# Dense stage of a streaming encoder step: U's products in three rounded passes, fewer buffers, one tile's sums kept in PSUM

## The chip, the cores and the metric

One core of one Trainium2 chip runs the whole program in one launch. The metric is the device time of that launch in microseconds (us), the median of the runs taken. The core has five engines that run side by side, each with its own instruction queue in program order: TensorE (PE, with its weight loads shown as PEld), VectorE (DVE), ScalarE (ACT), GpSimd (POOL) and SyncE (SP). They meet only through semaphores. Transfers that SP and POOL issue run on 16 shared DMA engines.

## The reference, cut to what matters

The program computes one layer: RMSNorm, two kinds of attention, a gated merge, and then a PEER block, a retrieval over 16384 one-neuron experts. Only the PEER block matters here:

```
xn = rmsnorm(x)                                 # 1024 features
e, g = top-16 experts and softmax weights per head, 8 heads     # 128 experts per token
h = u[e] . xn                                   # hidden value of each chosen expert
a = gelu(h) * g
out = sum over e of a * v[e];  y = rmsnorm_final(x + out)
```

There are nine tiles of 128 tokens. `peer_u` and `peer_v` are 16384 x 1024 in float32. The final sums of all tiles, and the keys and values of the attentions, are outputs.

## The kernel before, in words

The stages before the last one (projection, attention, merge, routing) take the first 1905 us. The last stage is the function `dense`, and the change lies there, but for two small things: the early loads in the stage before it, and the list of buffers that are carried over.

`dense` does two jobs at once, for eight of the nine token tiles.

The **dense job** (four tiles, 512 tokens) multiplies by all experts. There are 128 blocks of 128 experts. For each block b, `hidden` (line 2466) forms the 128 x 512 hidden values on PE: eight matmuls of 128x512 in float32 over the feature chunks of `xd`. ACT applies Gelu (line 2448), giving a tile `A`. DVE multiplies `A` by the gates from `G` (line 2375, function `gate`), which are zero for tokens that did not choose the expert. Four blocks make a group (32 groups). `values` (line 2474) multiplies a group's four `A` tiles by V: eight chunks per group (four token tiles times two halves of the features), each four matmuls into one of four PSUM banks. DVE adds each finished chunk into `qacc` in SBUF (line 2384, function `take`). PE's order is: `hidden` of block b, then two chunks of `values` of the group before.

The **fetched job** (four tiles, 128 tokens each) gathers, for each token column slot, one row of u and v per partition. POOL issues one indirect transfer of 1 MB per slot (line 2315) into a ring of eight slots. DVE multiplies the u half with `xn` and sums it (line 2353, `products`), ACT applies Gelu to two columns (line 2438), DVE scales by the gate weight (line 2362) and adds the v half into the tile's sum (line 2367, `add_rows`), then frees the slot. There are 128 slots per tile, 512 in all.

Both jobs are woven into one **body step** per block, 128 in all. DVE's queue for block b (function `body`, line 2386) is: `gate` of block b-1, two `take`s, `products` of two slots, `add_rows` of the two slots before, `products` of two, `add_rows` of two. So each step holds four slots of the fetched job. ACT's step is: small Gelu, Gelu of the block, small Gelu. All engines hold eight steps in the body of a loop (line 2250). A tile of the fetched job is 32 steps; DVE's and ACT's loops end there and `tile_done` finishes the tile. The eight steps of the first body are written out; the other fifteen bodies run in four loops, one per tile, so a loop is left for the last time at each tile's end.

SP (line 2258) loads U blocks into four buffers `ub`, V into two sets of four, and the gates of a group (1 MB) into one of two buffers `gb`. The first four U blocks and V blocks were loaded already in the stage before. A U buffer is free again when PE's `hidden` of the block four earlier is done. At the stage's end SP stores `qacc`.

Of the kernel before, what the change touches and what calls it, by code (L numbers as in the profile page):

```python
# [1332 lines left out]
def decide(nc, a, o, software, acc, aw, row_v, ring, w_o, dense_in):  # L1333
# [27 lines left out]
    with ExitStack() as ctx:  # L1361
# [76 lines left out]
        with nc.Block() as block:  # L1438
            @block.sync
            def _(sp):  # L1440
# [128 lines left out]
                for j in range(4):  # L1569
                    sp.dma_start(ring[:, j].rearrange("p (c q) -> p c q", q=P), a["u_blocks"][j]).then_inc(early_in, 16)  # L1570
                    sp.dma_start(ring[:, 4 + j], a["v_blocks"][j]).then_inc(early_in, 16)
# [5 lines left out]
                sp.wait_ge(early_in, 192)  # L1577
# [622 lines left out]
def dense(nc, a, o, soft, early, dense_in):  # L2200
# [7 lines left out]
    LEAD = 2 * DENSE  # L2208
    with ExitStack() as ctx:
# [9 lines left out]
        xn, acc = dense_in.xn, [dense_in.acc, sb("d_acc1", [P, D])]  # L2219
        gf = sb("d_gf", [P, D])  # L2220
        idx8 = [sb(f"d_idx8{u}", [P, SL], I32) for u in range(2)]
        h, ge, aw = (sb(f"d_{n}", [P, P]) for n in ("h", "ge", "aw"))
# [3 lines left out]
        HB, VB, SPARE = 0, 2, 6  # L2226
        wide = lambda b: ps[:, b:b + 2, :].rearrange("p b n -> p (b n)")

        tabs, rows_in, qacc_in = sem("d_tabs"), sem("d_rows_in"), sem("d_qacc_in")
        gf_in = sem("d_gf_in")  # L2230
        u_in = [sem(f"d_u_in{j}") for j in range(GB)]
        v_in, g_in = [sem(f"d_v_in{u}") for u in range(2)], [sem(f"d_g_in{u}") for u in range(2)]
# [23 lines left out]
        with nc.Block() as block:  # L2256
            @block.sync
            def _(sp):

                def u_rows(b, j):  # L2260
                    if not (number(b) and b < GB):
                        sp.wait_ge(h_done, b - GB + 1)
                        sp.sem_inc(sp_past, 1)
                    sp.dma_start(ub[j], a["u_blocks"][b]).then_inc(u_in[j], 16)
# [4 lines left out]
                def group(n, u, beside=lambda j: None):  # L2269
                    if not (number(n) and n < 2):  # L2270
                        sp.wait_ge(gated, GB * (n - 1))
                        sp.sem_inc(sp_past, 1)
                    sp.dma_start(gb[u][:], o["G"][bass.ts(n, GB)].rearrange("b p t -> p b t")).then_inc(g_in[u], 16)
                    for j in range(GB):
                        u_rows(GB * n + j, j)
                        if j == 0 and not (number(n) and n < 2):
                            sp.wait_ge(v_done, 2 * DENSE * (n - 1))
                            sp.sem_inc(sp_past, 1)
                        v_rows(GB * n + j, u, j)
                        beside(j)  # L2280

                for j in range(GB):
                    sp.sem_inc(u_in[j], 16)  # L2283
                sp.sem_inc(v_in[0], 16 * GB)
                sp.dma_start(gb[0][:], o["G"][0:GB].rearrange("b p t -> p b t")).then_inc(g_in[0], 16)
                sp.dma_start(gw[:], o["gw"].rearrange("t p s -> p t s")).then_inc(tabs, 16)
                sp.dma_start(idx[:, 1:], o["idx"][1:].rearrange("t p s -> p t s")).then_inc(rows_in, 16)

                def sums(j):
                    if j == 1:  # L2290
                        sp.dma_start(qacc[:], o["ys"][0:DENSE].rearrange("t p d -> p t d")).then_inc(qacc_in, 16)
# [3 lines left out]
                group(1, 1, sums)  # L2295
                with sp.Fori(1, NG // 2) as i:
                    for u in range(2):
                        group(2 * i + u, u)
                for q in range(DENSE):
                    sp.wait_ge(scaled, FETCHED + q + 1)  # L2300
                    sp.dma_start(o["y"][q], qacc[:, q]).then_inc(qy_st, 16)
# [4 lines left out]
            def _(pool):  # L2306
                def gathers(T, g, par):

                    nc.gpsimd.tensor_copy(idx8[par][:], idx[:, T, bass.ts(g, SL)]).then_inc(idx_copied, 1)
# [15 lines left out]
                for T in range(FETCHED):  # L2325
                    halves = P // SL // 4
                    if T == 1:
# [284 lines left out]
```

## Time and profile before

| what | value |
| --- | --- |
| median of 3 runs | 3753.05 us (3747.15 to 3762.25) |
| the profiled execution's own time | 3756.75 us |
| its span, first to last instruction | 3755.0 us |
| mean granted TensorE clock | 0.958 of full speed |
| PE busy | 3435.2 us, 91% of the span |
| DVE busy | 2662.5 us, 71% |
| ACT busy | 890.0 us, 24% |
| POOL busy | 1447.1 us, 39% |
| moved by DMA | 1201.16 MB, mean 320 GB/s |

How to read it: busy shares are averages over the span, and the last stage starts at about 1906 us. Matmuls are pipelined, so two that follow each other overlap in the records; the spacing of their starts tells more than the duration of one. "Idle before" gives the time for which the engine stood still just before an instruction, and the name behind it what ended that. "issue" there means that the profile shows nothing that the engine waited for. A wait of an engine that is not the bottleneck costs nothing.

### The profile page before, as it was taken

The page shows a single profiled execution, that of the slowest core. Times are in us where ns is not written, and L with a number is a line of the kernel's source. Part 1 is how long each engine was busy: PE and PEld are TensorE (multiplying, and loading weights), DVE is VectorE, ACT ScalarE, POOL GpSimd, SP SyncE. Part 2 cuts the span into 40 slices and gives each one's busy share as a digit, 9 for nine tenths or more (in the row PEclk, how much of TensorE's full clock was granted, in tenths as well). Part 3 has the DMA queues.
Part 4 walks back from the last instruction along what each step waited for, and adds up shares of the span by engine and source line. Part 5 has one row for each costly group of instructions (what it writes and reads, how often), then busy time and mean ns, then how long its engine had stood idle before and what let it go on. Part 6 is the DMA issues. An engine that isn't in the chain of part 4 may idle for free.

```text
span 3755.0 us, 45250 instructions
## 1 busy us (share of the span) xinstructions
PE 3435.2 (91%) x14374; PEld 2026.9 (54%) x14374; DVE 2662.5 (71%) x4988; ACT 890.0 (24%) x1844; POOL 1447.1 (39%) x1116
## 2 busy tenths in 40 slices
PE   8998989986889998999549999999999999999998
PEld 7444879884466667677414444444444444444443
DVE  0453887756368755655768888887888888889786
ACT  1452211215122338797100000100001000100001
POOL 0000187740232778874023343333343334333331
PEclk8899999988899999999779999999999999999999
DMA  7898499975887668888679999999999999999994
GB/s 262 342 421 298 136 401 378 378 275 168 322 311 252 170 179 182 193 147 190 205 285 398 406 398 390 398 390 391 409 385 400 406 397 418 401 399 365 387 379 185
DMA packets 470727, 1201.16 MB, mean 320 GB/s; under 512 B 196953, under 2 KB 261897, under 8 KB 391817
## 3 DMA queue, kind: packets, MB, share of 16 engines
q0 software_dynamic: 149776, 679.68, 47.7%
q1 hardware_dynamic: 187200, 498.50, 35.7%
q10 hardware_dynamic: 133568, 20.84, 3.5%
q8 instruction: 80, 1.31, 0.1%
q14 instruction: 103, 0.84, 0.1%
HBM read 1127.33 MB, written 72.61 MB: 320 GB/s over the span
## 4 chain that ended last, share of the span: by engine, by line
PE 32%; DVE 8%; issue 4%; DMA 4%; DVEq 1%; POOL 1%; POOLq 0%
PE d_ps L2482 17%; PE d_ps L2471 15%; DVE d_acc L2367 4%; DMA d_ring<-peer_uv,d_idx 3%; DVE d_ring L2353 3%; DMA out_y<-k_yacc 1%; DVE d_qacc L2384 1%; DVE k_yacc L2367 1%; POOL d_ring L2315 0%; DVE d_aw L2362 0%; DVE d_a L2375 0%; DVE d_qacc L2413 0%; DVEq L2362 0%; DVEq L2353 0%; DVEq L2366 0%
## 5 line engine op out<-in xcount | busy, mean ns | idle before, releaser
L2315 POOL DMA_INDIRECT d_ring<-peer_uv,d_idx x512 | 654.3, 1278 | 1067.1 <-DVEq L2369 964.1
L2471 PE MATMUL d_ps<-k_xd,k_ring 128*128 128x512 f32 x2048 | 907.0, 596 | 74.6 <-SPq L2283 60.4
L2471 PEld LDWEIGHTS d_ps<-k_xd,k_ring 128*128 128x128 f32 x2048 | 391.5, 191 | 569.4 <-issue 508.3
L2353 DVE SCALAR_TENSOR_TENSOR d_ring<-d_ring,k_xn 128x1024 f32<-128x1024 f32 x512 | 605.6, 1219 | 70.2 <-DMA d_ring<-peer_uv,d_idx 39.5
L2482 PE MATMUL d_ps<-d_v,d_a 128*128 128x512 f32 x1024 | 456.9, 600 | 32.5 <-DVE d_a L2375 24.6
L2482 PE MATMUL d_ps<-k_ring,d_a 128*128 128x512 f32 x1024 | 451.7, 594 | 16.1 <-DVE d_a L2375 16.1
L1630 POOL DMA_INDIRECT G<-c_cellg,c_cell x256 | 420.2, 1641 | 116.8 <-issue 90.1
L2367 DVE SCALAR_TENSOR_TENSOR d_acc<-d_ring,d_aw,d_acc 128x1024 f32<-128x1024 f32 x256 | 328.8, 1284 | 49.9 <-DVE d_acc L2367 32.3
L2367 DVE SCALAR_TENSOR_TENSOR k_yacc<-d_ring,d_aw,k_yacc 128x1024 f32<-128x1024 f32 x256 | 328.7, 1284 | 47.8 <-DVE k_yacc L2367 31.7
L2482 PEld LDWEIGHTS d_ps<-d_v,d_a 128*128 128x128 f32 x1024 | 196.3, 193 | 284.7 <-issue 283.4
L2438 ACT ACTIVATE d_ge<-d_h (+1 forms) x256 | 52.1, 203 | 1238.6 <-DVE d_ring L2353 1238.5
L2482 PEld LDWEIGHTS d_ps<-k_ring,d_a 128*128 128x128 f32 x1024 | 195.1, 191 | 262.5 <-issue 262.0
L2142 PE MATMUL c_ps<-c_mT,c_chunk 128*128 128x128 f32 x2048 | 250.2, 283 | 23.6 <-DMA c_chunk<-wq 22.5
L2142 PEld LDWEIGHTS c_ps<-c_mT,c_chunk 128*128 128x128 f32 x2048 | 244.6, 199 | 29.3 <-DMA c_chunk<-wq 24.2
L934 POOL DMA_INDIRECT k_merge<-peer_uv,a_rowu x128 | 168.9, 1319 | 193.7 <-DVE k_rowv L1002 148.1
L2384 DVE TENSOR_TENSOR d_qacc<-d_ps,d_qacc 128x512 f32<-128x512 f32 x256 | 167.5, 683 | 49.0 <-PE d_ps L2482 41.6
L1024 DVE SCALAR_TENSOR_TENSOR k_merge<-k_merge,k_xg 128x1024 f32<-128x1024 f32 x128 | 152.8, 1223 | 51.9 <-DMA k_merge<-peer_uv,a_rowu 47.0
L1094 PE MATMUL a_ps<-a_w_high,k_x_part 128*128 128x256 f32 x896 | 166.9, 288 | 1.8 <-issue 1.7
L1596 POOL DMA_INDIRECT k_ring<-peer_uv,k_rowv x56 | 66.9, 1195 | 219.7 <-DVE k_acc L1800 98.7
L2375 DVE TENSOR_TENSOR d_a<-d_a,d_gb 128x512 f32<-128x512 f32 x128 | 88.5, 691 | 80.3 <-issue 50.2
L1094 PEld LDWEIGHTS a_ps<-a_w_high,k_x_part 128*128 128x128 f32 x896 | 143.2, 196 | 3.0 <-issue 2.6
L1094 PE MATMUL a_ps<-a_w_low,k_x_part 128*128 128x256 f32 x448 | 129.1, 288 | 11.0 <-ACT a_stage L1051 9.1
(382 smaller groups left out, 4442.3 us busy)
## 6 DMA issues: line engine op xcount, KB each, us to landing
c_chunk<-wq SPq DMA_DIRECT2D x128, 512.0 KB
k_ring<-u_blocks SPq DMA_DIRECT2D x128, 512.0 KB, 12.7
s_kc<-sb_kT SPq DMA_DIRECT2D x32, 1024.0 KB, 9.1
s_vc<-sb_v SPq DMA_DIRECT2D x32, 1024.0 KB, 7.3
c_chunk<-w_m SPq DMA_DIRECT2D x64, 512.0 KB
k_ring<-v_blocks SPq DMA_DIRECT2D x64, 512.0 KB, 13.4
d_gb<-G SPq DMA_DIRECT2D x32, 1024.0 KB
d_v<-v_blocks SPq DMA_DIRECT2D x64, 512.0 KB
```

The lines of the kernel that those rows point to most:

```text
L934: pool.indirect_dma_start(out=ring[:, k % RB], out_offset=None, in_=rows, in_offset=bass.IndirectOffsetOnAxis(ap=source[:, k % P:k % P + 1 ...
L1024: nc.vector.scalar_tensor_tensor(ring[:, r], ring[:, r], 1.0, xg[:], ALU.mult, ALU.mult, accum_out=h_sb[:, s:s + 1]).then_inc(freed, 1)
L1094: last = nc.tensor.matmul(out, lhsT(left, k), rhs(right, k), start=(k == 0 and n == 0), stop=(k == KC - 1 and n == 2))
L1630: pool.indirect_dma_start(out=grid, out_offset=bass.IndirectOffsetOnAxis(ap=cell[q][:, s:s + 1], axis=0), in_=cell_g[q][:, s:s + 1], in_of ...
L2142: last = nc.tensor.matmul(ps[:, QUERY[w // 4], (w % 4) * P:(w % 4 + 1) * P], wq[:, c * P:(c + 1) * P], xT[:, c], start=(c == 0), stop=(c = ...
L2315: pool.indirect_dma_start(out=ring[:, b], out_offset=None, in_=a["peer_uv"], in_offset=bass.IndirectOffsetOnAxis(ap=idx8[par][:, b:b + 1], ...
L2353: last = nc.vector.scalar_tensor_tensor(ring[:, b, 0:D], ring[:, b, 0:D], 1.0, xn[T % 2][:], ALU.mult, ALU.mult, accum_out=h[:, bass.ds(co ...
L2367: nc.vector.scalar_tensor_tensor(acc[T % 2][:], ring[:, b, D:], aw[:, bass.ds(col + n, 1)], acc[T % 2][:], ALU.mult, ALU.add).then_inc(sum ...
L2375: nc.vector.tensor_tensor(A[u][j][:], A[u][j][:], gb[u][:, j], ALU.mult).then_inc(gated, 1)
L2384: nc.vector.tensor_tensor(part, ps[:, VB + c % 4, :], part, ALU.add).then_inc(v_taken, 1)
L2471: last = nc.tensor.matmul(ps[:, HB + x % 2, :], ub[j][:, k], xd[:, k].rearrange("p t q -> p (t q)"), start=(k == 0), stop=(k == KC - 1))
L2482: last = nc.tensor.matmul(ps[:, VB + c % 4, :], A[u][j][:, q * P:(q + 1) * P], vb[u][j][:, half * 512:half * 512 + 512], start=(j == 0), s ...
```

## The change

- U's products run in three passes in the type float32r. `x_high` is a rounded copy of the dense tokens, `x_low` what is missing to the full value; both are made once at the stage's start (ACT copies, DVE subtracts, 128x2048 at a time, two of each). For every block ACT makes `u_high` (128x1024, `high`) and DVE makes `u_low` = U - `u_high` (128x1024, `low`). PE then does eight times (`u_high` x `x_high`, `u_high` x `x_low`) and, once `u_low` is there, eight times `u_low` x `x_high`. There is one `u_high` and one `u_low`, so ACT's `high` of block b waits until PE has used and DVE has read the last one, and DVE's `low` of b waits until PE has finished b-1.
- Two U buffers in place of four; one is free when `low` has read it. Only two U blocks are loaded in the stage before.
- The gates lie in two buffers of half a group each (512 KB), in the space of the two U buffers.
- `A` lies in the space of `xd`, which is spent once `x_high` and `x_low` are made.
- The fourth token tile's two chunks (c = 6, 7) stay in PSUM over all 32 groups and are added to the tile once, at the end, so `take` runs for six chunks of a group and not eight. The bank pair that ACT's `square_sum` wrote to is gone; it writes to a spent `xn` buffer.
- Slot lists and gate weights of the fetched job are loaded per tile by POOL, half a tile ahead, and not all at once by SP.

```diff
-        ub = [early[:, j].rearrange("p (c q) -> p c q", q=P) for j in range(GB)]
+        ub = [early[:, s].rearrange("p (c q) -> p c q", q=P) for s in range(2)]
+        u_high, u_low = (sb(f"d_u_{part}", [P, KC, P], F32R) for part in ("high", "low"))
+        x_high, x_low = (sb(f"d_x_{part}", [P, KC, Q], F32R) for part in ("high", "low"))
-        gb = [sb(f"d_gb{u}", [P, GB, Q]) for u in range(2)]
-        A = [[sb(f"d_a{u}{j}", [P, Q]) for j in range(GB)] for u in range(2)]
-        qacc = sb("d_qacc", [P, DENSE, D])
+        gb = [early[:, 2 + s].rearrange("p (b t) -> p b t", t=Q) for s in range(2)]
+        A = [[x_all[:, GB * u + j] for j in range(GB)] for u in range(2)]
+        qacc = sb("d_qacc", [P, DENSE - 1, D])
 # SP
                 def u_rows(b, j):
-                        sp.wait_ge(h_done, b - GB + 1)
-                    sp.dma_start(ub[j], a["u_blocks"][b]).then_inc(u_in[j], 16)
+                    sp.wait_ge(u_low_done, b - 1)
+                    sp.dma_start(ub[j % 2], a["u_blocks"][b]).then_inc(u_in[j % 2], 16)
 # POOL, half way through each tile
                         pool.dma_start(xn[(T + 1) % 2][:], o["xn"][T + 1]).then_inc(xn_in, 16)
+                        pool.dma_start(idx[:, (T + 1) % 2], o["idx"][T + 1]).then_inc(xn_in, 16)
+                        pool.dma_start(gw[:, (T + 1) % 2], o["gw"][T + 1]).then_inc(xn_in, 16)
 # DVE
+                def low(b, j):
+                    dve.wait_ge(u_high_done, b + 1)
+                    if not (number(b) and b == 0):
+                        dve.wait_ge(h_done, b)
+                    nc.vector.tensor_tensor(u_low[:], ub[j % 2], u_high[:].bitcast(F32), ALU.subtract).then_inc(u_low_done, 1)
                 def take(n, c):
+                    if c >= KEPT:
+                        return
 # DVE body, after gate of b-1 and before the takes
+                        low(b, j)
 # ACT
+                def high(b, j, round):
+                    act.wait_ge(u_in[j % 2], 16 * (round + 1))
+                    if not (number(b) and b == 0):
+                        act.wait_ge(high_used, b)
+                        act.wait_ge(u_low_done, b)
+                    nc.scalar.activation(u_high[:], ub[j % 2], ACT.Copy).then_inc(u_high_done, 1)
 # ACT body, ahead of the first small Gelu
+                        high(b, j, 4 * k + x // 2)
 # PE
                     for k in range(KC):
-                        last = nc.tensor.matmul(ps[:, HB + x % 2, :], ub[j][:, k], xd[:, k].rearrange("p t q -> p (t q)"), start=(k == 0), stop=(k == KC - 1))
+                        for n, x_part in enumerate((x_high, x_low)):
+                            last = nc.tensor.matmul(ps[:, HB + x % 2, :], u_high[:, k], x_part[:, k], start=(k == 0 and n == 0), stop=False)
+                    last.then_inc(high_used, 1)
+                    pe.wait_ge(u_low_done, b + 1)
+                    for k in range(KC):
+                        last = nc.tensor.matmul(ps[:, HB + x % 2, :], u_low[:, k], x_high[:, k], start=False, stop=(k == KC - 1))
                     last.then_inc(h_done, 1)
```

## Rows read from the trace of the kernel before

**Rows 1.** The page: busy time by engine; the chain's share by engine.

```profile
PE 3435.2 (91%) x14374; PEld 2026.9 (54%) x14374; DVE 2662.5 (71%) x4988; ACT 890.0 (24%) x1844; POOL 1447.1 (39%) x1116
PE 32%; DVE 8%; issue 4%; DMA 4%; DVEq 1%; POOL 1%; POOLq 0%
```

**Rows 2.** Windows of the dense stage: busy us by engine, clock, DMA share, GB/s.

```profile
2908.00:3018.00 110.00, 110.00 (x258) 48.77 (x257) 95.67 (x137) 9.21 (x25) 42.86 (x36) 1.00 1.01 407
2457.00:2569.00 112.00, 110.18 (x257) 48.56 (x256) 94.79 (x136) 9.20 (x25) 42.80 (x36) 1.00 0.99 395
```

**Rows 3.** Timeline of PE: start, length, instruction, count (16: half a step).

```profile
2430.94 7.03 PE L2471 MATMUL d_ps<-k_xd,k_ring 128*128 128x512 f32 x16
2437.80 7.03 PE L2482 MATMUL d_ps<-k_ring,d_a 128*128 128x512 f32 x16
```

**Rows 4.** Timeline of DVE over one step, from gate to gate, same columns.

```profile
2430.81 0.69 DVE L2375 TENSOR_TENSOR d_a<-d_a,d_gb 128x512 f32<-128x512 f32 x1 [0.23 <-DVE d_acc L2367]
2431.42 1.28 DVE L2384 TENSOR_TENSOR d_qacc<-d_ps,d_qacc 128x512 f32<-128x512 f32 x2
2432.62 1.22 DVE L2353 SCALAR_TENSOR_TENSOR d_ring<-d_ring,k_xn 128x1024 f32<-128x1024 f32 x1
2433.76 0.08 DVE L2353 DVE_READ_ACCUMULATOR d_ring<-d_ring,k_xn  x1
...
2443.93 0.69 DVE L2375 TENSOR_TENSOR d_a<-d_a,d_gb 128x512 f32<-128x512 f32 x1 [0.23 <-DVE d_acc L2367]
```

**Rows 5.** Chain that ended last, 2400 to 2600 us: start, length, what.

```profile
2474.01 5.93 issue
2481.96 4.10 DVE d_ring L2353 x7
```

**Rows 6.** Timeline of PE, three passes in float32r in the projection.

```profile
440.07 0.62 PE L1094 MATMUL a_ps<-k_x_part,a_w_high 128*128 128x512 f32 x2
...
440.75 0.62 PE L1094 MATMUL a_ps<-k_x_part,a_w_high 128*128 128x512 f32 x2
```

**Rows 7.** Lines that split high and low parts: ns min/median/max; and a 128x1024 copy.

```profile
L944 DVE TENSOR_TENSOR a_w_low<-k_merge,a_w_high x11: 2284/2292/2312, 395.9 to 796.4; 128x2048 fp32r<-128x2048 f32 x11
L1056 ACT ACTIVATE a_w_high<-k_merge x11: 1915/1917/1923, 393.9 to 761.2; 128x2048 fp32r<-128x2048 f32 x11
L1949 ACT ACTIVATE c_mT<-c_y 128x1024 f32<-128x1024 f32 x8 | 8.3, 1043 | 14.3 <-DVE c_y L1675 14.3
```

**Rows 8.** Waits of DVE, 2034 to 3690 us: total, times, longest.

```profile
DVE d_a L2375 <- issue: 50.2, 8, 6.8
DVE d_qacc L2384 <- PE d_ps L2482: 18.2, 31, 3.6
DVE d_ring L2353 <- DMA d_ring<-peer_uv,d_idx: 10.9, 8, 2.8
```

**Rows 9.** Timeline of DVE at a loop's return: a slow one, one of third tile.

```profile
2480.15 0.69 DVE L2375 TENSOR_TENSOR d_a<-d_a,d_gb 128x512 f32<-128x512 f32 x1 [6.41 <-issue]
...
2926.17 0.69 DVE L2375 TENSOR_TENSOR d_a<-d_a,d_gb 128x512 f32<-128x512 f32 x1 [0.71 <-DVE k_yacc L2367]
```

**Rows 10.** Timeline of DVE at the stage's start, first gathered slots.

```profile
1917.19 1.22 DVE L2353 SCALAR_TENSOR_TENSOR d_ring<-d_ring,k_xn 128x1024 f32<-128x1024 f32 x1 [11.10 <-DMA d_ring<-peer_uv,d_idx]
1935.02 1.23 DVE L2353 SCALAR_TENSOR_TENSOR d_ring<-d_ring,k_xn 128x1024 f32<-128x1024 f32 x1 [1.39 <-DMA d_ring<-peer_uv,d_idx]
```

**Rows 11.** PE after a long stand, and clock (before last two) of the window.

```profile
2709.25 4.05 PE L2482 MATMUL d_ps<-d_v,d_a 128*128 128x512 f32 x5 [6.21 <-DVE d_a L2375]
2704.00:2712.00 8.00, 2.75 (x4) 1.21 (x5) 3.59 (x6) 0.00 (x0) 0.60 (x2) 0.61 1.02 421
2480.99 1.55 PE L2482 MATMUL d_ps<-d_v,d_a 128*128 128x512 f32 x3 [1.82 <-DVE d_a L2375]
```

**Rows 12.** The page: U's transfers of 512 KB, us from issue to landing.

```profile
k_ring<-u_blocks SPq DMA_DIRECT2D x128, 512.0 KB, 12.7
```

**Rows 13.** Line of the gate: ns min/median/max, first and last start.

```profile
L2375 DVE TENSOR_TENSOR d_a<-d_a,d_gb x128: 683/691/693, 1931.8 to 3715.5; 128x512 f32<-128x512 f32 x128
```

More of the change, by code:

```diff
@@ L2197, in _, with dense @@
                 scores_of(NT - 1)
-def dense(nc, a, o, soft, early, dense_in):
+def dense(nc, a, o, soft, spent_acc, early, dense_in):
     GB = 4
@@ L2280, in group @@
                         beside(j)
[L2282 removed]
+                for j in range(2):
                     sp.sem_inc(u_in[j], 16)
                 sp.sem_inc(v_in[0], 16 * GB)
[L2285 to L2287 removed]
+                for s in range(2):
+                    gates(0, s)
@@ L2296, in _ @@
-                with sp.Fori(1, NG // 2) as i:
+                group(0, 0, beside=sums)
+                group(1, 1)
+                with sp.Fori(1, NG // 2 - 1) as i:
                     for u in range(2):
                         group(2 * i + u, u)
+                group(NG - 2, 0)
+                group(NG - 1, 1, last=True)
+                sp.wait_ge(scaled, FETCHED - 1)
+                sp.dma_start(xn[0][:], o["ys"][DENSE - 1]).then_inc(held_in, 16)
                 for q in range(DENSE):
@@ L2419, in tile_done @@
                     if T + 1 < FETCHED:
-                        dve.wait_ge(xn_in, 16 * (T + 1))
+                        dve.wait_ge(xn_in, 48 * (T + 1))
                         dve.wait_ge(acc_in, 16 * (T + 1))
+                dve.wait_ge(x_high_done, KC)
+                for half in range(2):
+                    part = slice(half * KC // 2, (half + 1) * KC // 2)
+                    nc.vector.tensor_tensor(x_low[:, part], x_all[:, part], x_high[:, part].bitcast(F32), ALU.subtract).then_inc(x_low_done, 1)
                 bodies(dve, body, tile_done)
@@ L2428, in _ @@
                     take(NG - 1, c)
+                dve.wait_ge(held_in, 16)
+                for half in range(2):
+                    dve.wait_ge(v_done, 2 * DENSE * NG)
+                    part = xn[0][:, half * 512:(half + 1) * 512]
+                    nc.vector.tensor_tensor(part, ps[:, HELD + half, :], part, ALU.add).then_inc(v_taken, 1)
                 for q in range(DENSE):
-                    finish(FETCHED + q, qacc[:, q])
+                    finish(FETCHED + q, totals[q])
             @block.scalar
@@ L2458, in tile_done, with hidden @@
                     square_sum(T, acc[T % 2][:], summed, P * (T + 1))
+                for half in range(2):
+                    part = slice(half * KC // 2, (half + 1) * KC // 2)
+                    last = nc.scalar.activation(x_high[:, part], x_all[:, part], ACT.Copy)
+                    last.then_inc(x_high_done, KC // 2)
                 bodies(act, body, tile_done)
                 for q in range(DENSE):
-                    square_sum(FETCHED + q, qacc[:, q], v_taken, LEAD + 2 * DENSE * (NG - 1) + 2 * q + 2)
+                    square_sum(FETCHED + q, totals[q], v_taken, LEAD + KEPT * (NG - 1 if q < DENSE - 1 else NG) + (2 * q + 2 if q < DENSE - 1 else 2))
             @block.tensor
             def _(pe):
-                def hidden(b, x, j, round):
-                    pe.wait_ge(u_in[j], 16 * (round + 1))
+                def hidden(b, x, j):
+                    if number(b) and b == 0:
+                        pe.wait_ge(x_high_done, KC)
+                        pe.wait_ge(x_low_done, 2)
+                    pe.wait_ge(u_high_done, b + 1)
                     if not (number(b) and b < 2):
```

96 lines of the change are left out of this document (56 added, 40 removed).

## The prediction, made before the result was known

> **What bounds the kernel now.** I read the page first, then the windows of the last stage, then the two timelines of one body step, and last the chain and the waits. The page makes PE the bound: busy 91% against 71% for DVE, and the chain that ended last lies 32% on PE and 8% on DVE [rows 1]. The share of DVE is an average over stages, so the reader should next look at the dense stage alone. In a stretch of 110 us PE is busy all of it, DVE 95.67 us, and the DMA engines are at a share of 1.01 with 407 GB/s [rows 2]. Three resources are near their end together.
>
> The two timelines settle which one is first. PE's half step for U, 16 records, starts at 2430.94 and the next half at 2437.80 [rows 3]: 6.86 us, so 0.43 us for each record, and 13.72 us for a step of two halves. DVE's step runs from the gate at 2430.81 to the gate at 2443.93 [rows 4]: 13.12 us, and the idle time in it (0.23 us before a gate) follows DVE's own instructions. So DVE's step is a chain of DVE work that is only 0.60 us shorter than PE's. DVE has a second cost: when its loop returns, the gate starts after 6.41 us of idle time that nothing outside explains [rows 9], and the chain shows it as 5.93 us of "issue" between pieces of DVE work [rows 5]. It happens 8 times for 50.2 us together [rows 8]. In the third tile's loop the return costs 0.71 us [rows 9]. Eight steps with a slow return are 8 x 13.12 + about 6.4 = 111.4 us, eight steps of PE 109.8 us. The window of 112 us spans eight steps with such a return, and PE is busy only 110.18 us of it [rows 2]. DVE's four loops return 11 times, three times each but for the first tile's with two; without the third tile that leaves the 8. So in three of four tiles DVE is already the bound by 1 to 2 us in 110; only in the third tile is PE. That is the opposite of what the page suggests.
>
> **The change, part by part.**
>
> *PE.* A step's U half is now 8 x 3 products of 128x512 in float32r. The projection does just this: two products of one sort and one of the other repeat from 440.07 to 440.75 [rows 6], 0.68 us for three, so 8 x 0.68 = 5.44 us in place of 6.86. PE's step falls from 13.72 to 12.30 us; 128 x 1.42 = 182 us less PE work. The V half is the same. On the path this is worth only what DVE now waits for PE. DVE waits 18.2 us for chunks inside the stage [rows 8]; that is all that can be given back, and I take all of it.
> By the Trainium skill (FP8 and Floating Point Precision, TensorE Precision Notes) full float32 takes four passes through the array, of high and low parts; three of four would make U's half 5.15 us and the saved PE work 219 us. The row's 5.44 us for three passes is measured, and it decides.
>
> *DVE, added.* `low` is a 128x1024 subtraction from SBUF and SBUF. The same operation on 128x2048 takes 2.29 us [rows 7], and a 128x1024 instruction keeps DVE for 1.14 us, from 2432.62 to 2433.76 [rows 4]. Half of 2.29 is 1.15. I take 1.14: 128 x 1.14 = 146 us. Its two waits are resolved in the queue while the gate runs, as those of the takes are, which follow the gate with no idle time [rows 4]. From both sides: 0.60 us (a 128x512 one, from 2431.42 to 2432.62 for two) would be 77 us, with an idle time like the gate's 0.23 on top, 1.37 us, 175 us.
>
> *DVE, removed.* Two of eight takes per group go, 64 in all. Two takes hold DVE from 2431.42 to 2432.62 [rows 4], 0.60 us each: 64 x 0.60 = 38 us less. The last two, added at the end, are as long as the two that they replace: nothing.
>
> *DVE's step.* 13.12 + 1.14 - 0.30 = 13.96 us, against 12.30 for PE. DVE becomes the bound everywhere, by 1.66 us a step.
>
> *The waits that are added.* `low` of b waits for `u_high` of b and for PE's b-1. Behind it on DVE stand the takes and the four slots, so its lateness would cost in full. ACT makes `u_high` (about 1.04 us, as the 128x1024 copy [rows 7]) right after the small Gelu that follows DVE's last `products`. DVE then still has `add_rows` of two slots and the gate, over 3.5 us, against 1.3 us for ACT: hidden. PE's b-1 was done before the Gelu that DVE's gate of b-1 waited for: nothing. Behind `high` on ACT stand the small Gelu and the block's Gelu, which have some 3 us of room. Between 0 and 0.5 us a step (64 us) for such slips; I take 0.
> PE does the high passes before `low` is done, the last eight products (1.8 us) behind it, then 6.86 us of V. That ends about 9 us after `low`, some 5 us before the next takes want the chunks.
>
> *Startup.* The splitting of x takes two copies of 1.92 and two subtractions of 2.29 us [rows 7], and then the first `low`: 9.6 us after the stage's start. DVE waits 11.10 us there for its first slot anyway [rows 10]. If that cover were gone, it would cost 5.7 us of DVE. In the first four steps DVE also waits for slots, 1.39 us before one product [rows 10] and longer before others; three `low`s, 3.4 us, vanish in it. I count 4 us.
>
> *Loads.* A U block is now fetched once `low` of two blocks earlier is done, and ACT wants it nearly two steps later, 25 us. It lands in 12.7 us by the page's median [rows 12]. SP issues more evenly than before. With the DMA engines near their limit [rows 2] it may be late now and then: 0 to 15 us, taken as 0. POOL issues two more small loads in each of three tiles, behind a slack that eight slots of lead give: 0. A longer step lowers the demand on the DMA engines, which should give back some of the 10.9 us that DVE waits for slots [rows 8]; with the stalls in the middle of a tile I take 8 us.
>
> *The loop's return.* DVE's loop grows by some twenty instructions. The three quick returns of the third tile can become slow: 3 x 5.7 = 17 us (6.41 less 0.71 [rows 9]); all could also become quick, 8 x 5.7 = 46 us less. I take the 17, since three of four loops are slow now and the loop only grows.
> The Trainium skill (Runtime: NRT & Kernel Launch, Instruction fetch mechanics) says that a taken branch to a target outside the two blocks of instructions held on chip stalls for their fetch. The trace agrees in kind, with 6.41 us, and the rule also speaks for a longer loop being worse.
>
> *TensorE's clock.* While DVE's loop returns, PE now stands still for over 6 us, since `low` comes behind the return. In the trace before, after a stand of 6.21 us the granted clock is 0.61 on average over the window around it, which is the lower level of 1.2 GHz for most of it; stands of 1.82 us leave it at 2.4 GHz [rows 11]. After each of 11 returns and 3 tile ends PE is then 3 to 7 us behind, and 5 us are covered. I take 11 x 0.5 + 3 x 1 = 8 us; from 0 to 14 x 4 = 56 us.
>
> *Sum.* 146 - 38 - 18 - 4 - 8 + 17 + 8 = +103 us. The profiled execution took 3756.75 us for a span of 3755.0; 3756.75 + 103 = 3860. The median of the runs is 3.7 us lower, so the predicted median is 3856, some 2.7% slower. The tail adds nothing: after the last gate PE has the same 8 chunks to do as now.
>
> **The rivals.**
>
> *A, faster: PE is the bound, and the subtraction goes into DVE's idle time.* For it: PE's 91% and 32% of the chain [rows 1], and the window where PE is busy all of the time [rows 2]. It decides from the point where DVE's step is longer than PE's; it would need DVE's 13.12 us to hold over 1.1 us of wait for PE. Then the limit would be the DMA engines: 5.5 MB a step (four slots, U, V, a quarter of G) at 407 to 421 GB/s is 13.1 to 13.5 us [rows 2, 11], against 14.04 us for a step with all returns now (1783.7 us from the first gate to the last, 127 steps [rows 13]). At 13.2 us that is 127 x 0.84 = 107 us less: about 3650 us. Against it: DVE's unbroken step [rows 4] and its place in the chain [rows 5]. 9%.
>
> *B, little slower: the returns all become quick.* Then +103 - 17 - 46 - 8 = +32, about 3785 us. For it: the third tile does it already [rows 9]. 8%.
>
> *C, much slower: the single `u_high` and `u_low` chain the engines together.* ACT's `high`, PE's passes, DVE's `low` and the Gelu then form one loop that is longer than DVE's step, and PE's gaps bring the lower clock often. It decides once PE's stands in each group pass the lengths of rows 11. With 1 us more per step, +128 us, it is about 3985 us. Against it: the 3.5 us of cover above. 10%.
>
> The likeliest case has 73%. Its own range is 3805 to 3895 us: the 17 us of the returns and the 56 of the clock either way, and 18 us of waits that may not go. The range for 8 in 10 is 3775 to 3915: it takes in B, not A and not most of C. Under 0.5% (19 us) a measurement of this kernel does not tell from no change. Faster by more than that: A and a small rest, 10%. Within it: the low end of B, 5%. Slower: 85%.
>
> **What would show it.** Right: the gates of DVE 13.9 to 14.0 us apart within a loop; `low` at 1.2 us with a spacing of 1.14 us and no idle time before it; the group of U's products with idle time before it that DVE's `u_low` ends; three float32r products in 0.68 us; the line of the takes waiting for PE hardly at all; 8 to 11 "issue" waits of about 6 us on DVE; the chain mostly on DVE in this stage. Wrong: idle time before `low` that ACT's `u_high` or PE ends (C); gates under 13.5 us apart (A); long waits of `high` for U's transfers, which would mean that two buffers are too few; a step where ACT's copy brings a table load with it and Gelu comes late.

## The result, and the profile after

| | before | after |
| --- | --- | --- |
| median | 3750.1 us (3745.92 to 3762.25, 4 runs) | 3869.43 us (3863.2 to 3871.33, 4 runs) |
| the profiled execution's own time, its span | 3756.75, 3755.0 us | 3867.84, 3866.1 us |
| mean granted clock | 0.958 | 0.939 |

The ratio is 1.0308, with a 95% interval of 1.0293 to 1.0324: 119 us slower between the medians, 111 us between the two profiled executions. The forecast had 103 us on the profiled execution and 3856 us for the median.

The page after, in the two lines that answer to [rows 1]: busy time by engine, and the chain's share.

```profile
PE 3334.4 (86%) x15398; PEld 2233.8 (58%) x15398; DVE 2773.1 (72%) x5056; ACT 1032.4 (27%) x1986; POOL 1542.8 (40%) x1122
DVE 28%; issue 10%; PE 9%; DVEq 3%; DMA 1%; ACT 0%; POOL 0%; POOLq 0%; ACTq 0%
```

PE has lost 101 us of busy time and DVE gained 111. DVE's busy share went from 71% to 72% only, while its share of the chain went from 8% to 28%: the shares of busy time don't show who is the bound; the chain does here, and as the experiments show it did before (PE 32%, DVE 8% [rows 1]), where I read past it. The same stretches as in [rows 2], columns as there:

```profile
2908.00:3018.00 110.00, 95.53 (x292) 56.38 (x291) 93.07 (x127) 17.21 (x32) 43.95 (x33) 0.95 0.96 370
2457.00:2569.00 112.00, 98.08 (x301) 58.92 (x300) 94.21 (x132) 16.10 (x30) 44.85 (x33) 0.94 0.95 364
```

PE, busy in all 110 us before, now stands for 14 of them, and the DMA engines move 370 GB/s in place of 407. No engine is full any more, which is how a chain of dependences on one engine looks in such a table: what DVE lacks to 110 us are the small gaps between its own instructions and the return of its loop. DVE after, gates and what follows them (answers to [rows 4]):

```profile
2536.20 0.69 DVE L2407 TENSOR_TENSOR k_xd<-k_xd,k_ring 128x512 f32<-128x512 f32 x1 [0.22 <-DVE k_acc L2392]
2536.81 1.22 DVE L2401 TENSOR_TENSOR d_u_low<-k_ring,d_u_high 128x1024 fp32r<-128x1024 f32 x1
2537.95 1.28 DVE L2418 TENSOR_TENSOR d_qacc<-d_ps,d_qacc 128x512 f32<-128x512 f32 x2
...
2550.48 0.69 DVE L2407 TENSOR_TENSOR k_xd<-k_xd,k_ring 128x512 f32<-128x512 f32 x1 [0.22 <-DVE k_acc L2392]
...
2564.75 0.69 DVE L2407 TENSOR_TENSOR k_xd<-k_xd,k_ring 128x512 f32<-128x512 f32 x1 [0.22 <-DVE k_acc L2392]
2577.91 0.69 DVE L2407 TENSOR_TENSOR k_xd<-k_xd,k_ring 128x512 f32<-128x512 f32 x1 [0.31 <-DVE k_acc L2392]
```

The gates are 14.27 us apart where the step has takes and 13.16 where it has none, one step in four: 13.99 on average, against 13.12. `low` sits between the gate and the takes, costs 1.14 us (2536.81 to 2537.95) and has no idle time before it. PE in the same kernel: the first product of a U half, its last eight, the V half and the next U half:

```profile
2442.60 0.50 PE L2532 MATMUL d_ps<-d_x_high,d_u_high 128*128 128x512 f32 x1 [1.56 <-ACT d_u_high L2486]
...
2446.33 2.08 PE L2536 MATMUL d_ps<-d_x_high,d_u_low 128*128 128x512 f32 x8
2448.26 7.03 PE L2549 MATMUL d_ps<-k_ring,k_xd 128*128 128x512 f32 x16
2455.61 0.50 PE L2532 MATMUL d_ps<-d_x_high,d_u_high 128*128 128x512 f32 x1 [0.33 <-ACT d_u_high L2486]
```

U's half takes 5.66 us in place of 6.86 in [rows 3], and then PE waits 1.56 or 0.33 us for the next `u_high`, which itself waits for DVE: PE's step would be some 12.5 us, and it is given 13.2 to 14.3. The waits of DVE from the first gate to the last, which answer to [rows 8] (total, times, longest; beside the line with "u_high" DVE waits for ACT only at the tiles' ends, 11.4 us as before):

```profile
DVE k_xd L2407 <- issue: 78.2, 11, 11.7
DVE d_qacc L2418 <- PE d_ps L2549: 18.7, 15, 2.7
DVE d_ring L2378 <- DMA d_ring<-peer_uv,d_idx: 1.2, 1, 1.2
DVE d_u_low L2401 <- ACT d_u_high L2486: 0.8, 3, 0.3
```

One return of the loop on DVE, and the same in the chain that ended last (answers to [rows 5, 9]):

```profile
2502.49 1.28 DVE L2392 SCALAR_TENSOR_TENSOR k_acc<-d_ring,k_scores,k_acc 128x1024 f32<-128x1024 f32 x1 [0.26 <-DVE k_acc L2392]
2510.34 0.69 DVE L2407 TENSOR_TENSOR k_xd<-k_xd,k_ring 128x512 f32<-128x512 f32 x1 [6.57 <-issue]
```
```profile
2504.04 6.06 issue
```

Nine of the eleven returns are like it, 5.7 to 7.3 us of idle time. The first tile's two are longer, 10.8 and 11.7 us:

```profile
2269.98 0.69 DVE L2407 TENSOR_TENSOR k_xd<-k_xd,k_ring 128x512 f32<-128x512 f32 x1 [11.65 <-issue]
```

"issue" means that the profile shows nothing that the engine waited for, but the view of the DMA queues shows what arrived meanwhile. Taken over the idle time alone, q14, a queue that carries nothing but instructions, moved one packet of 8 KB in the return at 2510.34 and two in the one at 2269.98; in the quick returns of the third tile in the kernel before it moved none. Its line for each of the two, in this order (queue, packets, MB, share of the 16 engines):

```profile
q14 instruction: 1, 0.01, 0.3%
q14 instruction: 2, 0.02, 0.3%
```

So it is in all 88 returns of the eight kernels here whose DVE loops return: none in the nine quick ones (0.7 us), one or two in the 79 slow ones (3.5 to 12.2 us), two in each of the 17 that are over 10 us. I read the slow returns as stands for DVE's own instructions. No run takes the packets away and keeps the loop, and why a return needs none, one or two is not shown.

PE at the return of 2510.34, and the window around it, with the granted clock ahead of the last two columns:

```profile
2500.34 0.79 PE L2532 MATMUL d_ps<-d_x_high,d_u_high 128*128 128x512 f32 x1 [3.29 <-ACT d_u_high L2486]
2500.92 0.63 PE L2532 MATMUL d_ps<-d_x_low,d_u_high 128*128 128x512 f32 x1
2501.35 0.63 PE L2532 MATMUL d_ps<-d_x_high,d_u_high 128*128 128x512 f32 x1
...
2512.22 3.78 PE L2536 MATMUL d_ps<-d_x_high,d_u_low 128*128 128x512 f32 x8 [5.22 <-DVE d_u_low L2401]
```
```profile
2498.00:2518.00 20.00, 12.45 (x29) 8.79 (x30) 10.59 (x14) 3.77 (x5) 5.59 (x5) 0.66 0.96 358
```

DVE stands 6.57 us. PE stood 3.29 us before it, does 16 products, stands 5.22 us for `u_low`, and its products are 0.43 us apart in place of 0.23: the clock is at 1.2 GHz for two thirds of these 20 us. It is so around each return. From 1960 us on, the low level holds for 203 us after, 42 us before.

The line of the gate closes the account (answers to [rows 13]):

```profile
L2407 DVE TENSOR_TENSOR k_xd<-k_xd,k_ring x128: 684/692/694, 1924.2 to 3825.5; 128x512 f32<-128x512 f32 x128
```

From first to last gate it is 1901.3 us against 1783.7, +117.6. The first gate comes 7.6 us earlier (5.0 of them in stages ahead of this one, which the change hardly touches) and the tail is 1.1 us longer: +111.1, the difference of the spans. The dense stage alone is thus 116 us longer.

### The profile page after: what moved, and what is told of

The parts are those of the page before. It is cut to its first block, busy times and chain, and to the rows that moved or that the text cites. A ratio compares the mean times of both kernels' runs of the same rounds, so it can differ in the third digit from the quotient of the medians.

```text
span 3866.1 us, 48207 instructions
## 1 busy us (share of the span) xinstructions
PE 3334.4 (86%) x15398; PEld 2233.8 (58%) x15398; DVE 2773.1 (72%) x5056; ACT 1032.4 (27%) x1986; POOL 1542.8 (40%) x1122
## 4 chain that ended last, share of the span: by engine, by line
DVE 28%; issue 10%; PE 9%; DVEq 3%; DMA 1%; ACT 0%; POOL 0%; POOLq 0%; ACTq 0%
DVE d_ring L2378 10%; DVE k_acc L2392 7%; DVE k_yacc L2392 7%; PE d_ps L2549 5%; DVE d_qacc L2418 3%; PE d_ps L2532 2%; PE d_ps L2536 2%; DVE d_u_low L2401 1%; DVEq L2387 1%; DMA d_ring<-peer_uv,d_idx 1%; DVE k_scores L2387 1%; DVEq L2378 0%; DVEq L2392 0%; DVEq L2391 0%; DVEq L2394 0%
## 5 line engine op out<-in xcount | busy, mean ns | idle before, releaser
L2532 PE MATMUL d_ps<-d_x_high,d_u_high 128*128 128x512 f32 x1024 | 443.3, 433 | 234.8 <-ACT d_u_high L2486 165.9
L2549 PE MATMUL d_ps<-d_v,k_xd 128*128 128x512 f32 x1024 | 460.1, 603 | 11.8 <-issue 11.8
L2549 PE MATMUL d_ps<-k_ring,k_xd 128*128 128x512 f32 x1024 | 449.8, 592 | 0.0
L2532 PE MATMUL d_ps<-d_x_low,d_u_high 128*128 128x512 f32 x1024 | 417.9, 408 | 0.0
L2532 PEld LDWEIGHTS d_ps<-d_x_high,d_u_high 128*128 128x128 f32 x1024 | 204.4, 200 | 358.2 <-ACT d_u_high L2486 160.8
L2392 DVE SCALAR_TENSOR_TENSOR k_acc<-d_ring,k_scores,k_acc 128x1024 f32<-128x1024 f32 x256 | 328.8, 1285 | 53.1 <-DVE k_acc L2392 35.5
L2392 DVE SCALAR_TENSOR_TENSOR k_yacc<-d_ring,k_scores,k_yacc 128x1024 f32<-128x1024 f32 x256 | 328.8, 1284 | 49.4 <-DVE k_yacc L2392 33.3
L2536 PE MATMUL d_ps<-d_x_high,d_u_low 128*128 128x512 f32 x1024 | 283.2, 422 | 89.8 <-DVE d_u_low L2401 89.5
L2549 PEld LDWEIGHTS d_ps<-d_v,k_xd 128*128 128x128 f32 x1024 | 200.2, 196 | 240.9 <-issue 234.8
L2532 PEld LDWEIGHTS d_ps<-d_x_low,d_u_high 128*128 128x128 f32 x1024 | 204.4, 200 | 48.4 <-issue 7.7
L2407 DVE TENSOR_TENSOR k_xd<-k_xd,k_ring 128x512 f32<-128x512 f32 x128 | 88.6, 692 | 108.1 <-issue 78.2
```

The source lines that it names most:

```text
L2392: nc.vector.scalar_tensor_tensor(acc[T % 2][:], ring[:, b, D:], aw[:, bass.ds(col + n, 1)], acc[T % 2][:], ALU.mult, ALU.add).then_inc(sum ...
L2532: last = nc.tensor.matmul(ps[:, HB + x % 2, :], u_high[:, k], x_part[:, k], start=(k == 0 and n == 0), stop=False)
L2536: last = nc.tensor.matmul(ps[:, HB + x % 2, :], u_low[:, k], x_high[:, k], start=False, stop=(k == KC - 1))
L2549: last = nc.tensor.matmul(ps[:, VB + c % 4 if c < KEPT else HELD + half, :], A[u][j][:, q * P:(q + 1) * P], vb[u][j][:, half * 512:half * ...
```

## The experiments

Differences in us are those of the ratios to the kernel before, measured beside each, times 3757. Theory D: DVE's instruction stream is the bound, so what counts is what is added to it and how often its loop returns. Rival P: PE is the bound, through its waits and its low clock.

**One pass less on PE** (the product's `x_low` part is left out).

```
-                        for n, x_part in enumerate((x_high, x_low)):
+                        for n, x_part in enumerate((x_high,)):
```

> The changed kernel without the passes of U's high part by x_low, so that U's products are two passes; all else as it is. The first theory (DVE's own queue sets the step, 14.27 us with takes and 13.16 without) says that 8 x 0.227 = 1.8 us less PE work per step gives nothing within the loops, and at most 15 us through quicker catching up after the loop's returns: 3854 to 3870 us. The rival (PE, or the chain ACT's u_high, PE's passes, DVE's u_low, sets the step) says 128 x 1.8 = 232 us less, or at least half of it: under 3755 us.

3857.79 us, 1.0272 (1.0251 to 1.0294): 14 us less than the changed kernel. PE does 216 us less, the gates stay 14.27 and 13.17 us apart. P is refuted for the changed kernel. PE's part behind the returns is small: of the profiled executions' difference 7.6 us lie between the first gate and the last, 6.7 of them in DVE's waits for PE.

**Half of the subtraction** (the last eight passes read the same half of `u_low` twice).

```
+                    nc.vector.tensor_tensor(u_low[:, 0:KC // 2], ub[j % 2][:, 0:KC // 2], u_high[:, 0:KC // 2].bitcast(F32), ...
```

> The changed kernel with u_low made for only half of the features, 128x512 in place of 128x1024; PE does all its passes, the last eight over the same half twice. The first theory says DVE's step is shorter by 1.14 - 0.60 = 0.54 us: 128 x 0.54 = 69 us less, 3800 us (3790 to 3810). The rival (PE or the chain over u_high sets the step) says no change from 3869 us.

3816.88 us, 1.0159 (1.0142 to 1.0176): 56 us less, 7 us above the expected range. DVE in this kernel, the two instructions around `low`:

```profile
2548.52 0.69 DVE L2407 TENSOR_TENSOR k_xd<-k_xd,k_ring 128x512 f32<-128x512 f32 x1 [0.22 <-DVE k_acc L2392]
2549.13 0.68 DVE L2401 TENSOR_TENSOR d_u_low<-k_ring,d_u_high 128x512 fp32r<-128x512 f32 x1
...
2561.15 0.69 DVE L2407 TENSOR_TENSOR k_xd<-k_xd,k_ring 128x512 f32<-128x512 f32 x1 [0.31 <-DVE k_acc L2392]
```

A step lost 0.53 us, 128 of them 68 us; DVE's waits for slots grew by 10 and for PE by 4. The step's cost arrives in full, less what a faster stream waits for others.

**Eight takes again** (the two extra go to the first tile's sums; the fourth tile's sum is left out).

```
-    KEPT = 2 * DENSE - 2
+    KEPT = 2 * DENSE
```

> The changed kernel with the fourth tile's chunks taken out of PSUM again for each group, eight takes in place of six; the two are added to the first tile's sums, and the fourth tile's sum is left out, as SBUF has no room for it. The first theory says 64 x 0.60 = 38 us more: 3907 us (3897 to 3917). The rival (PE or the chain sets the step) says under 10 us more.

3933.38 us, 1.0462 (1.044 to 1.0483): 58 us more than the changed kernel, 20 beyond the 38 expected. All steps are 14.27 us, as expected. The rest is in the returns, DVE's wait in this kernel:

```profile
DVE k_xd L2407 <- issue: 112.7, 11, 12.2
```

10.2 us on average for each return in place of 7.1, 34 us in all, with 380 instructions in DVE's loop (counted with those of its queue) in place of 370. The average mixes two sizes, and the tiles have changed sides: the first tile's two are 5.9 and 6.4 us, the other nine 10.5 to 12.2. One of the nine:

```profile
2654.33 0.69 DVE L2407 TENSOR_TENSOR k_xd<-k_xd,k_ring 128x512 f32<-128x512 f32 x1 [10.54 <-issue]
```

From the first gate to the last this kernel is 57 us longer than the changed one: 38 for the takes and 34 for the returns, less 11 of DVE's waits for PE (18.7 us there, 7.2 here); 4 us stay open. The profiled spans differ by 69 us, since the stages ahead took 12.7 us longer in this execution.

**The subtraction alone, put into the kernel before** (its output, in a spare PSUM tile, is not read).

```
+                        nc.vector.tensor_tensor(wide(SPARE), xn[T % 2][:], xn[T % 2][:], ALU.subtract)
```

> The kernel before with one more DVE instruction per step, a subtraction of 128x1024 float32 whose result nobody reads, and ScalarE's squares written to a spent buffer as in the changed kernel. The first theory (the kernel before was bound by DVE in three of four tiles, with 13.12 us against 13.72 for PE) says 128 x 1.14 = 146 us more, less the 18 us for which DVE waited for PE and some 4 at the start, and 17 more if the third tile's returns become slow: 3750 + 124 = 3874 us (3860 to 3895). The rival (PE bound the kernel before, and DVE had room) says under 40 us more.

3856.15 us, 1.0257 (1.0237 to 1.0277): 97 us more than before and 4 us under the expected range, over four fifths of the whole change with U's product still in full float32. Its waits on DVE from the stage's start:

```profile
DVE d_a L2375 <- issue: 49.6, 8, 6.6
DVE d_ring L2353 <- DMA d_ring<-peer_uv,d_idx: 27.6, 12, 10.3
DVE d_qacc L2384 <- PE d_ps L2483: 24.3, 8, 5.1
```

Steps are 14.26 us: 127 x 1.14 = 145, less 17 us of waits for PE and 12 for slots that it had from the stage's start on, and 3 of another wait: 113, and the spans differ by 107; 6 us stay open. The third tile's returns became slow, as I had predicted for the changed kernel, but the fourth tile's became quick:

```profile
3469.61 0.69 DVE L2375 TENSOR_TENSOR d_a<-d_a,d_gb 128x512 f32<-128x512 f32 x1 [0.75 <-DVE d_acc L2367]
```

So the returns don't simply get worse with the loop's length.

**DVE's loops written out in the changed kernel**, no returns.

```
+                    for i in range(1 if T == 0 else 0, TB // BODY):
+                        body(T, first + i)
```

> The changed kernel with VectorE's four loops written out, so that nothing returns; the other engines keep their loops. The first theory (the 11 returns stop DVE for 78 us in all and drag PE's clock down behind them) says the eight steps of a body take 2 x 13.16 + 6 x 14.27 = 111.9 us in place of 119 to 120, and the whole 80 to 100 us less than the changed kernel: 3770 to 3790 us. The rival (the time behind a return is spent anyway, as DVE would next wait for slots or for PE) says under 30 us less.

3725.84 us, 0.9924 (0.9899 to 0.995): 144 us less than the changed kernel, much more than expected. Gates in this kernel, in a step with takes:

```profile
2608.10 0.69 DVE L2411 TENSOR_TENSOR k_xd<-k_xd,k_ring 128x512 f32<-128x512 f32 x1 [0.22 <-DVE k_acc L2396]
2621.83 0.69 DVE L2411 TENSOR_TENSOR k_xd<-k_xd,k_ring 128x512 f32<-128x512 f32 x1 [0.22 <-DVE k_acc L2396]
```

13.73 us: in this order of instructions the loop costs 0.54 us in every step beside its returns. The idle time before sums and products that wait for the one before is 0.16 us each here and 0.26 in the loop. There the values waited for and the columns addressed are worked out from the loop's variable, and here they are constants; which of the two costs the time is not shown. From the first gate to the last it is 1760.9 us in place of 1901.3, 140 less: 78 of returns, 127 x 0.54 = 69 of steps, 9 of waits for PE and 5 of other "issue", less 21 by which DVE's waits for slots grew (1.2 to 22.7 us). Most of the other 8 us between the spans lie ahead of the first gate.

**The order product, sum, product, sum on DVE**, so that an instruction doesn't wait for the one right ahead of it; slots are given back one instruction later. Alone in the changed kernel, with the written-out loops in the kernel before, and with them in the changed kernel.

```
+                    last = product(T, hb, now[0], 0, col)
+                    free_owed()
+                        add_row(T, hb - 1, before[0], 0, col - 2)
+                    last = product(T, hb, now[1], 1, col)
```

> The changed kernel with DVE's four slot instructions of a half step in another order: product, add, product, add, and each slot freed after the next instruction, so that an add never waits for the one right before it. The idle time of 0.25 us before an add, a product or a gate that follows an add, four times a step, and 0.14 us behind the two weights, should go. The first theory says the steps fall from 14.27 and 13.16 us by about 1.1 us, until the DMA engines end it at 13.1 to 13.5 us a step on average: 90 to 130 us less, 3740 to 3780 us. The rival (PE or the chain over u_high sets the step) says no change.

3749.94 us, 0.9967 (0.9953 to 0.9982): 128 us less than the changed kernel, as expected. Two gates of this kernel, whose DVE loops still return:

```profile
2543.28 0.67 DVE L2435 TENSOR_TENSOR k_xd<-k_xd,k_ring 128x512 f32<-128x512 f32 x1
2555.72 0.67 DVE L2435 TENSOR_TENSOR k_xd<-k_xd,k_ring 128x512 f32<-128x512 f32 x1
```

The step is 12.44 us, 1.83 less than in the old order.

> The kernel before with both: DVE's loops written out, and the slot instructions woven. DVE's step would be 12.0 us, so PE with 13.72 us is the bound: 127 x 13.72 = 1742 us in place of 1784, some 40 us less, 3705 to 3720 us, PE busy without gaps. If the DMA engines are the bound already, it is less than 20 us.

3721.02 us, 0.9893 (0.9872 to 0.9915).

> The changed kernel with both: DVE's step would be 12.9 us and PE's 12.3 us, so the DMA engines come to be the bound at 13.1 to 13.5 us a step: 1670 to 1715 us from the first gate to the last in place of 1901 us, 3640 to 3685 us in all. Only here could the change pay: it would be 40 to 70 us under the kernel before with the same two edits (e7). If DVE is not relieved by the weaving, it stays near e5.

3703.45 us, 0.9852 (0.9832 to 0.9871): 15 us under the run before it, where 40 to 70 were expected. The first wait of DVE in each of these, in this order:

```profile
DVE d_ring L2385 <- DMA d_ring<-peer_uv,d_idx: 80.1, 77, 2.5
```
```profile
DVE d_qacc L2416 <- PE d_ps L2512: 227.0, 106, 4.9
```
```profile
DVE d_ring L2389 <- DMA d_ring<-peer_uv,d_idx: 120.7, 114, 5.2
```

With DVE relieved, the kernel before is bound by PE's float32 product (DVE waits for PE in 106 places), and the changed one mostly waits for the slots' transfers. Its undisturbed steps are 12.44 us with takes, as in the loop, so in this order the loop costs nothing beside its returns. From the first gate to the last its mean is 13.67 us a step (1736.3 us), over the 13.1 to 13.5 that I had expected of the DMA engines.

**In the kernel before, the fourth tile held in PSUM and nothing else.**

```
-                    if not (number(n) and n == 0 and c < 4):
+                    if c < KEPT and not (number(n) and n == 0 and c < 4):
```

> The kernel before with one part of the change alone: the fourth tile's sums stay in two PSUM banks through all groups, so that DVE makes six takes a group in place of eight and two at the end. U's products stay in full float32, no subtraction. Theory (DVE is the bound by 1 to 2 us in eight steps, PE right behind it): DVE's step goes from 13.12 to 12.82 us, PE's stays 13.72, so groups of eight steps fall from about 111.5 to 110 us and PE's full product becomes the bound; 11 to 20 us less in all, about 3740. Waits of takes for PE grow well past the 18 us of the kernel before. Rival (a take costs its full price on the path): 64 x 0.60 = 38 us less, about 3718. Rival (takes lie in idle time): nothing, 3755 to 3760.

3757.05 us, 1.0001 (0.9988 to 1.0013): nothing, against 11 to 20 us less. PE at a return, and DVE's waits, in this kernel:

```profile
2476.70 7.03 PE L2478 MATMUL d_ps<-k_xd,k_ring 128*128 128x512 f32 x16
2485.74 7.13 PE L2491 MATMUL d_ps<-d_v,d_a 128*128 128x512 f32 x16 [2.02 <-DVE d_a L2376]
2492.71 7.03 PE L2478 MATMUL d_ps<-k_xd,k_ring 128*128 128x512 f32 x16
```
```profile
DVE d_a L2376 <- issue: 50.7, 8, 6.8
DVE d_qacc L2387 <- PE d_ps L2491: 47.2, 50, 2.7
```

PE works without a gap except behind the return, where it stands 2.02 us for the gate; before, 1.82 us [rows 11]. Eight PE steps and this stand are 109.8 + 1.8 = 111.6 us, the distance that I had put down to eight DVE steps and a return (111.4). DVE's shorter stream only waits longer: for PE 47 us in place of 18, and for slots 50 in place of 39.5 from the stage's start on. No run makes PE's work shorter in the kernel before with DVE's stream left alone, so that PE was the bound rests on PE's unbroken work and on this run and the next.

**In the kernel before, DVE's loops written out and nothing else.**

> The kernel before with DVE's four loops of the stage written out, nothing else. Theory: DVE has no returns and its step is 12.6 us, so PE's 13.72 us is the bound in nearly all steps; 128 x 13.73 = 1757 us from the first gate to the last against 1783.7 us, about 27 to 37 us less: 3720 to 3730, as with the interleaved order on top of it (3721). Rival (the slots' transfers or PE's stands at tile ends, not DVE, make the rest): under 15 us less, 3743 or more.

3726.45 us, 0.9912 (0.9893 to 0.9932): 33 us less, as expected, with nearly all of its last stage's chain on PE (PE 46%, DVE 0% of the span), and with 105.6 us of takes that wait for PE. PE's stands at the eight slow returns in the kernel before (1.5 to 6.2 us each) add up to 25 of the 33 us.

**The store of a tile's output asked for earlier**, on top of both edits: in the changed kernel and in the one before. POOL in the changed kernel without this edit, at the middle of a tile:

```profile
2541.82 0.57 POOL L2350 DMA_DIRECT2D out_y<-k_yacc  x1
2557.68 0.55 POOL L2363 DMA_DIRECT2D k_xn<-xn  x1 [15.29 <-DMA out_y<-k_yacc]
```

```
-                    with pool.Fori(0, halves) as i:
+                    with pool.Fori(0, halves // 2) as i:
```

> The changed kernel with DVE's loops written out, interleaved products and sums, and the store of a tile's output asked for a quarter of a tile earlier on POOL's queue, so that the gathers of slots do not stand behind it. Theory: the 15 us for which POOL stands at each of the two or three middles of a tile reach DVE as 6 to 8 us each, so 5 to 15 us less than with the same kernel without this edit (3703): 3688 to 3698. If the DMA engines are at their limit throughout, the requests that come earlier win nothing: 3700 to 3705.

3688.49 us, 0.9811 (0.9791 to 0.983): 15 us less than without it, as expected.

> The kernel before with the same three edits. Theory: PE's full float32 product is the bound there (busy all of the time, 13.73 us a step), so POOL's stand does not reach the end: within 4 us of 3721. The difference to the changed kernel with the same edits, 20 to 30 us, is what three passes are worth once DVE has been relieved. If it falls by 8 us or more, PE was not the bound in those steps.

3721.52 us, 0.9905 (0.989 to 0.9921): no different from the same kernel without it, as expected; the changed kernel is 35 us faster with the same edits, where 20 to 30 were expected. The stretch of [rows 2], in the changed kernel with all three edits:

```profile
2908.00:3018.00 110.00, 102.12 (x320) 61.99 (x319) 99.28 (x143) 18.18 (x34) 42.34 (x40) 0.97 1.02 417
```

The DMA engines are at a share of 1.02 and 417 GB/s, while PE has 8 us left. That the DMA engines are now the bound is read from this and from the waits for slots; no run moved fewer bytes. This kernel beats the one before by 1.9% and the one changed by 4.8%.

What the change is worth thus depends on DVE: 3.1% slower in the loops as they are, no difference with them written out (0.9924 against 0.9912), 0.4% faster in the interleaved order (the intervals barely apart), and 0.9% faster (0.9811 against 0.9905, intervals apart) once the store is moved too.

## Why the prediction was right, and where its terms were off

- *PE's three passes.* 5.44 us for the U half was the forecast, 5.66 was measured, and that this wins nothing on the path was shown by taking a further pass away.
- *`low`.* 1.14 us, no idle time, 14.27 and 13.16 us for the steps, 13.99 on average against 13.96. Shown from both sides: half of it takes 56 us away, it alone adds 97.
- *Takes.* The 38 us are right for a kernel that DVE bounds: putting them back cost 38 and longer returns. In the kernel before the same edit is worth nothing.
- *Which engine was first.* Here the argument failed, and it was luck that the number took no harm. I read 8 x 13.12 + 6.4 = 111.4 us as DVE being the bound in three of four tiles. PE was, and DVE reached it only through the gate behind the return. The two sums agree by chance: only an edit of DVE's stream (nothing) and one of its returns (33 us) could tell them apart. The last of [rows 11], PE's stand of 1.82 us, pointed to it, and so did the chain of the page, PE 32% against DVE 8% [rows 1], which I took for misleading.
- *Waits for PE, -18.* They did not go: 18.2 us in 31 places became 18.7 in 15. The small ones in plain steps went, and new ones of up to 2.7 us came in the first step behind returns and tile ends, where PE comes late after its stands and at the low clock.
- *Slots, -8, and start, -4.* Together they gave more: 21.8 us of waits for slots from the first gate on became 1.2, and from the stage's start to the first gate it is 23.2 us in place of 25.8.
- *Returns, +17.* Mechanism right, the third tile's three became slow, 18 us. The total grew by 28 us (50.2 to 78.2), and nearly all of the other 10 is the first tile's two, which rose from 6.1 and 6.8 us to 10.8 and 11.7; the six of the second and fourth tile take 38.0 us in place of 37.3. That a return can also become longer was not in the prediction. In the kernel before with the subtraction alone, a loop eight instructions longer (349 for 341) had quick returns in the fourth tile, which the shorter one had not. The Trainium skill (Runtime: NRT & Kernel Launch, Instruction fetch mechanics) has a taken branch out of the two blocks held on chip stall for a fetch; the slow returns agree, each with one or two packets of instructions in it and the quick ones with none. The reading that I took from it, that a longer loop is only ever worse, does not hold in that run: by the rule the place of each loop against the blocks would count as well, which fits returns that differ by tile, but no run here moved a loop without changing it.
- *Loads, 0.* Two U buffers are enough: ACT never waits for a transfer of U, and U's transfers land sooner than in [rows 12].

```profile
k_ring<-u_blocks SPq DMA_DIRECT2D x128, 512.0 KB, 8.0
```

- *Clock, +8.* The low level holds for 161 us more. It costs DVE only what stands in its waits for PE, so the term can't be separated from the 18.7 us; that the two together (-18 + 8) should come out near nothing is a miss of about 10 us.
- *Sum from gate to gate.* 127 x 0.87 = 110 us for the step; +28 - 2 for returns and other "issue"; -21 slots; +1 PE and ACT: 116, and 117.6 were measured.
- *How near it came.* 103 us were forecast for what turned out to be 116 in the dense stage. The misses partly cancel: +3 for the step, +18 for the waits for PE that stayed and +11 for the returns against -11 for slots and start and -8 for the clock, whose cost lies in those waits.
- *Rivals.* A (PE the bound, about 3650) fell with the experiment on the passes; its limit of the DMA engines did show once DVE was relieved, at 417 GB/s. B (all returns quick) didn't happen; with no returns at all the gain was larger than B's, since in the old order the loop costs in each step too. C (one buffer chains the engines) fell: DVE waits 0.8 us for `u_high`.

## What to carry to other kernels

When two engines' steps are within 5% of each other, moving work from one to the other is not a saving until it is known which of them is the bound, and busy shares don't tell: read the chain, follow one step on each, then test with an edit that shortens only the one. A sum that fits the measured distance is no proof when the other engine's sum fits it as well. And a program loop on an engine that sets the pace has two prices. One is at its return, where packets on the DMA queue of the instructions tell a slow return from a quick one. The other is in each instruction that waits for the one right ahead of it (0.26 us in the loop, 0.16 written out), and it goes when such instructions are interleaved. Both are worth reading before the arithmetic is changed.

## What the hardware showed that was not expected

- A return of DVE's loop is 0.7 us of idle time when no packet of instructions arrives in it, 3.5 to 7.3 us with one (all but two of them over 5.2), and 10.5 to 12.2 with two (three returns had two packets and took 6.5 to 6.8). By tile, in the order of the tiles: 6, 6, 0.7, 6 us with 341 instructions (and with 329) in the loop; 6, 6, 6, 0.7 with 349; 11, 6, 6, 6 with 370; 6, 11, 11, 11 with 380. What decides is open: the place of a loop was not varied alone.
- Dependent DVE instructions stand 0.26 us apart in the loop and 0.16 us in written-out code; in the interleaved order there is no gap in either. Per step that is 0.54 us and, with the order, a further 1.3 (13.73 to 12.44).
- In the changed kernel the granted clock fell to 1.2 GHz around each return; in the one shown PE stood for 3.29 and for 5.22 us. Before the change it stayed at 2.4 GHz at the five slow returns where PE stood for 1.5 to 2.2 us [rows 11], and fell at the three where it stood for 4.7, 4.7 and 6.2 us.
